# The first unit of the long convolutions, placed between the last input projections

## The chip, the cores and the metric

The program runs on one core of a Trainium2 chip. Five engines work side by side and meet at semaphores: TensorE (PE, matrix products into PSUM), VectorE (DVE), ScalarE (ACT), GpSimd (Pool) and SyncE (SP), of which the last two only issue transfers in the part told of here. The metric is the time of one execution on the device, in microseconds, as the median of several; less is better.

## The reference

The reference is a two-layer model of 1024 tokens by 1024 channels in float32: a mixer and a mixture of experts, then a second block. The change is in the second block, in its branch of long convolutions. There a projection of 3 x 1024 channels goes through a short convolution of 3 taps, is cut into v, x1 and x2, and v is convolved with a filter as long as the sequence, twice, each time multiplied by a gate:

```python
hy = dwconv(hy, conv_b_w[l], conv_b_b[l], (HYENA_CONV // 2, HYENA_CONV - 1 - HYENA_CONV // 2))
v, x1, x2 = jnp.split(hy, HYENA_ORDER + 1, axis=-1)
filt = hyena_filters(S, filt_w1[l], filt_b1[l], filt_w2[l], filt_b2[l], filt_w3[l], filt_freq[l])
z = v.astype(f32)
for n, gate in enumerate((x1, x2)):
    k = bidir_kernel(filt[:, n, 0], filt[:, n, 1])
    z = gate.astype(f32) * fftconv(z, k, filt_bias[l, n])
...
def fftconv(u, k, bias):
    L = u.shape[1]
    U = jnp.fft.rfft(u, n=2 * L, axis=1)
    K = jnp.fft.rfft(k, axis=0)
    y = jnp.fft.irfft(U * K[None], n=2 * L, axis=1)[:, :L]
    return y + u * bias.astype(jnp.float32)
```

## The kernel before

**Input projections** (`hyena_inputs_phase`). 24 tiles of 128 channels, j = 0 to 23; the first 16 hold v and x1, tiles 16 to 23 hold x2. For each tile SP loads 0.5 MB of weights (line 3311), DVE splits them into an upper part and a rest (`split_w`), PE makes the product in 48 matmuls (`wide_product`), ACT copies it to `raw`, DVE makes the three taps of the short convolution in `conv` (lines 3437 and 3442), and Pool stores it (line 3296 for x2). Two buffers of each alternate.

**Filter steps.** After tiles 17 to 22 PE also makes 16 slices of the filters (`make_filter`, 4 matmuls each, two PSUM tiles `turned` in turn), DVE multiplies each by its decay (`decay_filter`, line 4142; the two with t = 0 have two small fixups more) and ACT stores every second one. `STEPS_AFTER` says how many stand after each of the last eight tiles. A step needs the decay of the step two before it.

**Long convolutions** (`hyena_phase`). Four passes: pass 0 and 1 are the first convolution for the two halves of the channels, 2 and 3 the second one. A pass has two halves of the frequencies (fh), and a unit is one such (pass, fh): PE makes four spectra of the input, U(n, fh), each of a chunk `u` that SP loads from memory into one of three buffers (line 4260, 0.5 MB); ACT copies each (line 4408); DVE joins them by butterflies, multiplies by the filter's spectra K and goes through the butterflies of the inverse (lines 3769 to 4500), 34.85 us in all, and counts up `h_ready`. For pass 0, K is loaded (line 4164, 2 MB), for pass 1 it is made on PE too and joined by DVE. With both units of a pass done, PE makes I(n), the inverse transform, in 8 banks of PSUM, and DVE multiplies each bank into a gated result (line 4442); a bank is used again when the result two before it has been taken. Each engine goes through a fixed order:

```python
program = [("U", 0, 0), ("U", 0, 1), ("U", 1, 0), ("K", 1, 0), ("K", 1, 1), ("I", 0, 0), ("U", 1, 1), ("U", 2, 0),
           ("I", 1, 0), ("U", 2, 1), ("U", 3, 0), ("K", 3, 0), ("K", 3, 1), ("U", 3, 1), ("I", 2, 0), ("I", 3, 0)]
```

DVE takes the units in the order (0,0), (0,1), (1,0), (1,1), ... and puts the results of pass 0, numbered 0 to 7 here, between the operations of unit (1,0), those of pass 1 between the operations of (2,0). Below, "unit (0,1)" is DVE's work and "U(0,1)" PE's.

## Time and profile before

| | |
|---|---|
| median of 3 runs | 3959.01 us (3958.61 to 3959.40) |
| the profiled execution's own time | 3965.33 us |
| its span | 3963.4 us |
| PE busy over the span | 3711.4 us (94%) |
| DVE busy | 2842.3 us (72%) |
| ACT, Pool busy | 1856.4 us (47%), 260.6 us (7%) |
| last projection ends, long convolutions begin on PE | 2224.6 us |
| DVE's unit (0,0) | 2239.65 to 2274.50 us |
| I(0) on PE | 2312.1 to 2340.5 us |
| I(1) begins on PE | 2398.7 us |

Times in us are counted from the span's start. The shares of the whole span say little here, since most of it is the two mixtures of experts; the change is in 2138 to 2400 us. An idle time in brackets behind a row of a timeline is that of the engine just before the instruction, with what ended it.

### The profile page before, as it was taken

To read this page: it belongs to the slowest core of one execution; us is meant where nothing else is said; L and a number is where in the kernel's file an instruction comes from. 1 tells how busy PE (TensorE), PEld (TensorE's weight loads), DVE (VectorE), ACT (ScalarE), POOL (GpSimd) and SP (SyncE) were. 2 spreads that over 40 slices of the span, in tenths; PEclk is the share of its full clock that TensorE was granted. 3 is DMA by queue.
4 is the path that set the end of the run, shared out by engine and by line. 5 is a ranking of instruction groups with operands and counts; after the bars stand their busy time and mean duration, and the time that the engine had idled before them with its cause. 6 is when DMAs were issued, how large, how long until landed. Compare 5 with 4: busy or idle time off the path is not lost. (4 is left out here: it accounts for less than half of the span.)

```text
span 3963.4 us, 42184 instructions
## 1 busy us (share of the span) xinstructions
PE 3711.4 (94%) x16780; PEld 2853.8 (72%) x16780; DVE 2842.3 (72%) x2581; ACT 1856.4 (47%) x1719; POOL 260.6 (7%) x281
## 2 busy tenths in 40 slices
PE   8989989799999799999999987899499999999998
...
GB/s 118 6 11 116 22 71 159 321 417 415 417 415 353 228 126 72 67 67 103 95 122 143 201 142 102 53 159 120 192 369 387 383 389 379 390 381 389 388 383 319
DMA packets 367168, 891.04 MB, mean 225 GB/s; under 512 B 21994, under 2 KB 118609, under 8 KB 357556
## 3 DMA queue, kind: packets, MB, share of 16 engines
...
q8 instruction: 97, 1.59, 0.2%
...
## 5 line engine op out<-in xcount | busy, mean ns | idle before, releaser
L2342 DVE TENSOR_TENSOR moe_w_rest<-moe_w_w,moe_upper 128x2048 fp32r<-128x2048 f32 x384 | 862.2, 2287 | 134.5 <-ACT moe_upper L2243 68.5
L2243 ACT ACTIVATE moe_upper<-moe_w_w 128x2048 fp32r<-128x2048 f32 x192 | 357.4, 1909 | 233.3 <-PE moe_y_ps L2207 87.2
L2342 DVE TENSOR_TENSOR moe_w_rest<-moe_w_w,moe_upper_w 128x2048 fp32r<-128x2048 f32 x192 | 430.4, 2282 | 14.5 <-ACT moe_upper_w L2261 14.3
L2261 ACT ACTIVATE moe_upper_w<-moe_w_w 128x2048 fp32r<-128x2048 f32 x192 | 357.5, 1910 | 117.3 <-PE moe_up_ps L2181 72.5
L2251 ACT ACTIVATE moe_upper<-moe_w_w 128x2048 fp32r<-128x2048 f32 x192 | 356.7, 1912 | 3.5 <-DMA moe_w_w<-in_w_up_dram 3.5
L2181 PE MATMUL moe_up_ps<-moe_upper,moe_x_upper 128*128 128x512 f32 x768 | 308.6, 402 | 0.0
L2181 PE MATMUL moe_gate_ps<-moe_upper,moe_x_upper 128*128 128x512 f32 x768 | 300.8, 392 | 4.7 <-DVE moe_x_rest L2355 4.7
L2181 PE MATMUL moe_gate_ps<-moe_upper,moe_x_rest 128*128 128x512 f32 x768 | 300.4, 391 | 0.0
L2181 PE MATMUL moe_gate_ps<-moe_w_rest,moe_x_upper 128*128 128x512 f32 x768 | 300.1, 391 | 0.0
L2181 PE MATMUL moe_up_ps<-moe_upper,moe_x_rest 128*128 128x512 f32 x768 | 300.1, 391 | 0.0
L2181 PE MATMUL moe_up_ps<-moe_w_rest,moe_x_upper 128*128 128x512 f32 x768 | 299.0, 389 | 0.0
L2207 PE MATMUL moe_y_ps<-moe_upper_w,moe_hidT_upper 128*128 128x512 f32 x760 | 295.9, 389 | 1.9 <-DVE moe_hidT_rest L2360 1.9
L2207 PE MATMUL moe_y_ps<-moe_upper_w,moe_hidT_rest 128*128 128x512 f32 x760 | 295.7, 389 | 0.0
L2207 PE MATMUL moe_y_ps<-moe_w_rest,moe_hidT_upper 128*128 128x512 f32 x760 | 295.7, 389 | 0.0
L2181 PEld LDWEIGHTS moe_gate_ps<-moe_upper,moe_x_upper 128*128 128x128 f32 x768 | 145.1, 189 | 35.7 <-DVE moe_x_rest L2355 5.5
L2181 PEld LDWEIGHTS moe_up_ps<-moe_upper,moe_x_rest 128*128 128x128 f32 x768 | 144.1, 188 | 31.9
L2181 PEld LDWEIGHTS moe_gate_ps<-moe_upper,moe_x_rest 128*128 128x128 f32 x768 | 145.0, 189 | 30.3
L2181 PEld LDWEIGHTS moe_gate_ps<-moe_w_rest,moe_x_upper 128*128 128x128 f32 x768 | 145.2, 189 | 30.1
L2207 PEld LDWEIGHTS moe_y_ps<-moe_upper_w,moe_hidT_upper 128*128 128x128 f32 x760 | 142.6, 188 | 32.2 <-DVE moe_hidT_rest L2360 2.7
L2181 PEld LDWEIGHTS moe_up_ps<-moe_w_rest,moe_x_upper 128*128 128x128 f32 x768 | 144.6, 188 | 27.5
L2207 PEld LDWEIGHTS moe_y_ps<-moe_upper_w,moe_hidT_rest 128*128 128x128 f32 x760 | 142.7, 188 | 29.6
L2207 PEld LDWEIGHTS moe_y_ps<-moe_w_rest,moe_hidT_upper 128*128 128x128 f32 x760 | 142.7, 188 | 29.5
...
## 6 DMA issues: line engine op xcount, KB each, us to landing
...
moe_w_w<-in_w_up_dram SPq DMA_DIRECT2D x64, 2048.0 KB, 11.0
moe_w_w<-in_w_down_dram SPq DMA_DIRECT2D x64, 2048.0 KB, 10.9
...
```

Of the source, the lines that this page charges most:

```text
L2181: last = nc.tensor.matmul(out[:, :], lhs[:, k, :], rhs[:, k, :], start=(k == 0 and n == 0), stop=(k == ND - 1 and n == 2))
L2207: last = nc.tensor.matmul(m.y_ps[:, h, :], lhs[:, k, :], rhs[:, k, bass.ts(h, BANK)], start=(start and k == 0 and n == 0), stop=(stop and ...
L2243: act.activation(half(upper1(c), h), half(weights.w1[c % 2], h), ACT.Copy).then_inc(m.w1_rounded, 1)
L2251: act.activation(half(upper3(c), h), half(weights.w3[c % 2], h), ACT.Copy).then_inc(m.w3_rounded, 1)
L2261: act.activation(half(upper2(i, c), h), half(weights.w2[c % 2], h), ACT.Copy).then_inc(m.w2_rounded, 1)
L2342: dve.tensor_tensor(half(rest, h), half(whole, h), half(upper, h).bitcast(F32), ALU.subtract).then_inc(done, 1)
```

## The change

The unit (0,0) is made inside the projections. The filter steps are set to four after each of tiles 17 to 20 and none after 21 and 22. After them PE makes U(0,0) into the same two PSUM tiles `turned` that the filter steps use, ACT copies it to `first_U`, and DVE makes the unit ahead of the convolutions of tiles 21, 22 and 23, of which the one of 21 and the split of the last weights stand inside it. `first_U` lies where the filter's operand was, `first_K` where the decay was, and `first_cross` in `rows`. SP loads first_K and, once the first spectrum is made, the fourth chunk. Semaphores of the long convolutions are made earlier, Pool waits for the first unit before its first gates, and the load of the inverse's table waits for the first unit's products. The body of the butterflies became a function, `unit_butterflies`, with the same instructions.

```diff
-            for i in range(N_NAT // 2 + 1, N_ALL // 2):
-                load(i)
-                next_tables.load_rows(sp, v_x1, i - N_NAT // 2 - 1)
+            load(N_NAT // 2 + 1)
+            for b in range(2):
+                next_tables.load_rows(sp, v_x1, b)
+            load(N_NAT // 2 + 2)
+            next_tables.load_rows(sp, v_x1, 2)
+            next_tables.load_first_k(sp)
+            load(N_NAT // 2 + 3, [0])
+            next_tables.load_last_rows(sp, v_x1)
+            load(N_NAT // 2 + 3, [1])
...
                             next_tables.make_filter(pe, s, turned_ps[s % 2])
+                        if j == N_NAT + UNIT_AFTER:
+                            next_tables.first_spectra(pe, turned_ps)
...
                             next_tables.store_filter(act, s, kept_of(s))
+                        if j == N_NAT + UNIT_AFTER:
+                            next_tables.copy_first(act, turned_ps)
...
+            def last_tiles(unit):
+                LAST = N_ALL - 1
+
+                def between(at):
+                    if at == 4:
+                        split_w(LAST, LAST // 2, 1)
+                    elif at == 5:
+                        convolve(LAST - 2, (LAST - 2) // 2, 1, False)
+                split_w(LAST - 1, LAST // 2, 0)
+                for b in NB:
+
+                    dve.wait_ge(next_tables.filt_stored[b], 16 * (NT // 2))
+                dve.wait_ge(next_tables.fwd_copied, RADIX)
+                unit_butterflies(unit, next_tables, 0, next_tables.first_K[:, :, :, :], next_tables.first_U[:, :, :, :], first_cross[:, :, :, :], HC,
+                                 (next_tables.k_loaded[0], 16), between, False)
+                convolve(LAST - 1, LAST // 2, 0, False)
+                convolve(LAST, LAST // 2, 1, False)
...
-STEPS_AFTER = (0, 3, 3, 3, 3, 2, 2, 0)
+STEPS_AFTER = (0, 4, 4, 4, 4, 0, 0, 0)
+UNIT_AFTER = 4
...
-        sp.wait_ge(m.filt_ready, len(FILTER_STEPS))
+        sp.wait_ge(m.product_ready, 1)
         sp.dma_start(m.inv[:, :, :, :, :], m.inverse).then_inc(m.inv_loaded, 16)
...
+    def load_first_k(m, sp):
+
+        sp.wait_ge(m.filt_ready, len(FILTER_STEPS))
+        sp.dma_start(m.first_K[:, :, :, :], m.spectra[PASSES[0][0], 0]).then_inc(m.k_loaded[0], 16)
+
+    def load_last_rows(m, sp, v_x1):
+
+        sp.wait_ge(m.fwd_made, 1)
+        sp.dma_start(m.u[0][:, :, :], residues(v_x1, RESIDUE[RADIX - 1], 0)).then_inc(m.u_loaded[0], 16)
+
+    def first_spectra(m, pe, outs):
+
+        pe.wait_ge(m.tr_loaded, 16 * HJ)
+        pe.wait_ge(m.filt_ready, len(FILTER_STEPS))
+        for i in range(RADIX):
+            pe.wait_ge(m.u_loaded[i % N_CHUNKS], 16 * (i // N_CHUNKS + 1))
+            if i >= 2:
+
+                pe.wait_ge(m.fwd_copied, i - 1)
...
-            if what == "U":
+            if what == "U" and (n, fh) != (0, 0):
...
-        pool.wait_ge(fwd_made, RADIX)
+        pool.wait_ge(h_ready, 1)
```

On VectorE, before: the convolutions of the last two tiles; now: what follows the convolution of tile 20 (`block_w_first` and `hyin_w` are the two weight buffers, the first holds even tiles; `hyin_conv` is a convolution). Before:

```order
L3437 TENSOR_SCALAR hyin_conv<-hyin_raw,hyin_vec 128x1024
L3442 SCALAR_TENSOR_TENSOR hyin_conv<-hyin_raw,hyin_vec,hyin_conv 128x1024 x2
L3437 TENSOR_SCALAR hyin_conv<-hyin_raw,hyin_vec 128x1024
L3442 SCALAR_TENSOR_TENSOR hyin_conv<-hyin_raw,hyin_vec,hyin_conv 128x1024 x2
L4416 UNCONDITIONAL_BRANCH
L3769 TENSOR_TENSOR hyena_U<-hyena_U 128x2x1024
L3774 SCALAR_TENSOR_TENSOR hyena_U<-hyena_U 128x2x1024
```

Now, from the split of tile 22's weights to the middle of the unit:

```order
L130 CAST block_w_first_upper<-block_w_first 128x1024
L133 TENSOR_TENSOR block_w_first_rest<-block_w_first,block_w_first_upper 128x1024
L3813 TENSOR_TENSOR hytab_first_U<-hytab_first_U 128x2x1024
L3818 SCALAR_TENSOR_TENSOR hytab_first_U<-hytab_first_U 128x2x1024
L3813 TENSOR_TENSOR hytab_first_U<-hytab_first_U 128x1024
L3818 SCALAR_TENSOR_TENSOR hytab_first_U<-hytab_first_U 128x1024
L4260 TENSOR_TENSOR hytab_first_U<-hytab_first_U 128x512
L3813 TENSOR_TENSOR hytab_first_U<-hytab_first_U 128x512
L3818 SCALAR_TENSOR_TENSOR hytab_first_U<-hytab_first_U 128x512 x2
L4285 TENSOR_TENSOR hyin_first_cross<-hytab_first_U,hytab_first_K 128x2048
L130 CAST hyin_w_upper<-hyin_w 128x1024
L133 TENSOR_TENSOR hyin_w_rest<-hyin_w,hyin_w_upper 128x1024
```

The unit stood behind the last two convolutions, which now stand behind it; the split of tile 23's weights came before the convolution of tile 22 and is now inside the unit.

On SP, the transfers from the weights of tile 20 to the second unit's chunks (`hytab_u` is a chunk of the input, `tmp_spectra` the filter's spectra in memory). Before:

```order
L3311 DMA block_w_first<-in_w_in_dram 128x8x128
L3311 DMA hyin_w<-in_w_in_dram 128x8x128
L4161 DMA hytab_u<-tmp_v_x 128x2x512
L3311 DMA block_w_first<-in_w_in_dram 128x8x128
L3311 DMA hyin_w<-in_w_in_dram 128x8x128
L4161 DMA hytab_u<-tmp_v_x 128x2x512
L4245 UNCONDITIONAL_BRANCH
L4260 DMA hytab_u<-tmp_v_x 128x2x512
L4164 DMA hyena_K<-tmp_spectra 128x4096
L4260 DMA hytab_u<-tmp_v_x 128x2x512 x4
```

Now:

```order
L3314 DMA block_w_first<-in_w_in_dram 128x8x128
L3314 DMA hyin_w<-in_w_in_dram 128x8x128
L4213 DMA hytab_u<-tmp_v_x 128x2x512
L4218 DMA hytab_first_K<-tmp_spectra 128x4096
L3314 DMA block_w_first<-in_w_in_dram 128x8x128
L4223 DMA hytab_u<-tmp_v_x 128x2x512
L3314 DMA hyin_w<-in_w_in_dram 128x8x128
L4378 UNCONDITIONAL_BRANCH
L4391 DMA hytab_u<-tmp_v_x 128x2x512 x4
L4245 DMA hyena_K<-tmp_spectra 128x4096
```

The fourth chunk of U(0,0) stood ahead of the 2 MB of spectra and now stands behind them and behind the weights of tile 22.

On PE, where the filter steps of tile 20 end (L4179 and L4180 are `make_filter`, L2751 the projection of tile 21), now:

```order
L4179 MATMUL hyin_turned<-hytab_w_parts_14099,hytab_hid_upper 128x512
L4180 MATMUL hyin_turned<-hytab_w_parts_14099,hytab_hid_rest 128x512
L4179 MATMUL hyin_turned<-hytab_w_parts_14099,hytab_hid_upper 128x512
L4180 MATMUL hyin_turned<-hytab_w_parts_14099,hytab_hid_rest 128x512
L4236 MATMUL hyin_turned<-hytab_u,hytab_tr 128x512 x16
L2751 MATMUL hyin_proj<-block_h_T_upper,hyin_w_upper 128x512
L2751 MATMUL hyin_proj<-block_h_T_rest,hyin_w_upper 128x512
```

The 16 matmuls of U(0,0) stood behind the projection of tile 23 before, at the head of those of line 4328.

## Rows read from the trace of the kernel before

**Rows 1.** Busy time by stretch; columns in its first line.

```profile
core 0: us, PE busy (x) PEld busy (x) DVE busy (x) ACT busy (x) POOL busy (x), PEclk, DMA share, GB/s
2138.50:2224.70 86.20, 83.03 (x354) 67.03 (x353) 50.54 (x48) 6.17 (x6) 3.21 (x6) 0.98 0.38 134
...
2239.70:2312.10 72.40, 69.04 (x160) 30.43 (x161) 70.62 (x55) 15.36 (x15) 1.46 (x2) 1.00 0.39 144
...
2342.80:2398.70 55.90, 25.34 (x60) 10.88 (x58) 54.45 (x46) 8.19 (x8) 1.45 (x2) 0.76 0.56 207
```

**Rows 2.** Waits of PE from 2138 to 2560 us: total, times, longest.

```profile
PE hyena_inv_ps L4366 <- DVE hyena_U L4500: 30.6, 1, 30.6
...
PE hyin_turned L4127 <- DVE hyin_rows L4142: 0.9, 2, 0.5
```

**Rows 3.** Timeline of PE: start, length, line, count, idle before it.

```profile
2224.56 13.90 PE L4328 MATMUL hyena_fwd_ps<-hytab_u,hytab_tr 128*128 128x512 f32 x32
2240.22 14.00 PE L4328 MATMUL hyena_fwd_ps<-hytab_u,hytab_tr 128*128 128x512 f32 x32 [1.76 <-DMA hytab_u<-tmp_v_x]
2257.06 14.00 PE L4328 MATMUL hyena_fwd_ps<-hytab_u,hytab_tr 128*128 128x512 f32 x32 [2.84 <-DMA hytab_u<-tmp_v_x]
...
2312.10 7.03 PE L4366 MATMUL hyena_inv_ps<-hyena_U,hytab_inv 128*128 128x512 f32 x16
2319.81 20.87 PE L4366 MATMUL hyena_inv_ps<-hyena_U,hytab_inv 128*128 128x512 f32 x48 [0.68 <-DVE hyena_z L4442]
2340.52 10.03 PE L4328 MATMUL hyena_fwd_ps<-hytab_u,hytab_tr 128*128 128x512 f32 x23
```

**Rows 4.** Timeline of DVE, last tile and first unit, then results 0 and 7.

```profile
2226.67 2.61 DVE L3442 SCALAR_TENSOR_TENSOR hyin_conv<-hyin_raw,hyin_vec,hyin_conv 128x1024 f32<-128x1024 f32 x2
2239.65 2.29 DVE L3769 TENSOR_TENSOR hyena_U<-hyena_U 128x2048 f32<-128x2048 f32 x1 [10.38 <-ACT hyena_U L4408]
...
2249.72 2.29 DVE L4480 TENSOR_TENSOR hyena_cross<-hyena_U,hyena_K 128x2048 f32<-128x2048 f32 x1
...
2273.81 0.69 DVE L4500 SCALAR_TENSOR_TENSOR hyena_U<-hyena_U 128x512 f32<-128x512 f32 x1
...
2319.06 0.69 DVE L4442 TENSOR_TENSOR hyena_z<-hyena_inv_ps,hyena_z 128x512 f32<-128x512 f32 x1
...
2342.82 0.69 DVE L4442 TENSOR_TENSOR hyena_z<-hyena_inv_ps,hyena_z 128x512 f32<-128x512 f32 x1
```

**Rows 5.** Timeline of PE: projection 17, then the first filter steps.

```profile
2127.47 0.48 PE L2751 MATMUL hyin_proj<-block_h_T_upper,hyin_w_upper 128*128 128x512 f32 x1
...
2138.45 0.39 PE L4127 MATMUL hyin_turned<-hytab_w_parts,hytab_hid_upper 128*128 128x512 f32 x1
...
2142.35 0.50 PE L4127 MATMUL hyin_turned<-hytab_w_parts,hytab_hid_upper 128*128 128x512 f32 x1 [1.90 <-DVE hytab_filt L4147]
...
2143.61 0.63 PE L2751 MATMUL hyin_proj<-block_h_T_upper,block_w_first_upper 128*128 128x512 f32 x1
```

**Rows 6.** Timeline of DVE, decays of the filter steps.

```profile
2144.18 0.68 DVE L4147 SCALAR_TENSOR_TENSOR hyin_rows<-hyin_rows,hytab_bias 1x512 f32<-1x512 f32 x1
...
2159.64 1.23 DVE L4142 TENSOR_TENSOR hyin_rows<-hyin_turned,hytab_decay 128x1024 f32<-128x1024 f32 x1 [0.23 <-PE hyin_turned L4128]
```

**Rows 7.** Busy time by stretch, columns as in Rows 1.

```profile
2144.00:2146.00 2.00, 2.00 (x6) 1.59 (x5) 1.97 (x4) 0.00 (x0) 0.00 (x0) 0.50 0.00 0
2254.00:2258.00 4.00, 1.16 (x3) 0.49 (x3) 3.90 (x4) 1.02 (x1) 0.00 (x0) 1.00 0.68 226
```

**Rows 8.** Timeline of SP, issues of the two spectra loads of the first pass.

```profile
2228.60 0.47 SPq L4164 DMA_DIRECT2D hyena_K<-tmp_spectra  x1
...
2244.36 0.47 SPq L4164 DMA_DIRECT2D hyena_K<-tmp_spectra  x1
```

**Rows 9.** Landing times of the stores of a finished tile (line 3296).

```profile
DMA to landing us min/median/max: 2.9/3.1/9.2
```

**Rows 10.** Landing times of the input chunks loaded at line 4260.

```profile
DMA to landing us min/median/max: 3.6/4.7/17.9
```

More of the change, by code:

```diff
@@ L3261, in hyena_inputs_phase @@
         nat = v_x1.rearrange("(t p) c -> p t c", p=P)
+        unit = []
         def steps_after(j):
@@ L3303, in _, with load @@
         def _(sp):
-            def load(i):
-                for b in NB:
+            def load(i, tiles=NB):
+                for b in tiles:
                     j = 2 * i + b
@@ L3415, in _, with convolve @@
             ends = Chain(dve, next_tables.end_step)
+            def convolve(j, i, b, turning):
+                dve.wait_ge(raw_ready, j + 1)
+                if not first(i):
+                    if turning:
+                        dve.wait_ge(turned, j - 1)
+                    else:
+                        dve.wait_ge(stored[b], 16 * i)
+                dve.tensor_scalar(conv[b][:, :], raw[b][:, 0:T], vec[:, bass.ds(j, 1)], vec[:, bass.ds(j + R_BIAS, 1)],
+                                  ALU.mult, ALU.add).then_inc(tap_done, 1)
+                for k in range(1, HY_TAPS):
+                    dve.wait_ge(tap_done, (HY_TAPS - 1) * j + k)
+                    dve.scalar_tensor_tensor(conv[b][:, :], raw[b][:, k:k + T], vec[:, bass.ds(j + k * N_ALL, 1)], conv[b][:, :],
+                                             ALU.mult, ALU.add).then_inc(conv_ready if k == HY_TAPS - 1 else tap_done, 1)
             def two_tiles(i, turning):
@@ L3419, in two_tiles @@
                     j = 2 * i + b
-                    if not first(j) and not (isinstance(j, int) and j == N_ALL - 1):
+                    if not first(j):
                         split_w(j + 1, i + b, 1 - b)
@@ L3449, in _ @@
             next_tables.sum_weights(dve)
-            for i in range(N_NAT // 2, N_ALL // 2):
+            for i in range(N_NAT // 2, N_NAT // 2 + 2):
                 two_tiles(i, False)
-        return Ends(proj_made, N_ALL, raw_ready, N_ALL, conv_ready, N_ALL, rows_ready, N_NAT, stored, 16 * (N_ALL // 2))
+            split_w(N_ALL - 3, N_NAT // 2 + 2, 1)
+            for s in steps_after(N_ALL - 4):
+                next_tables.decay_filter(ends, s, turned_ps[s % 2], kept_of(s))
+            convolve(N_ALL - 4, N_NAT // 2 + 2, 0, False)
+            unit.append(Chain(dve, next_tables.step))
+            last_tiles(unit[0])
+        return Ends(proj_made, N_ALL, raw_ready, N_ALL, conv_ready, N_ALL, rows_ready, N_NAT, stored, 16 * (N_ALL // 2), unit[0])
 class MergeStore(Store):
@@ L4063, in open @@
         m.k_loaded = [m.sem(f"k_loaded{fh}") for fh in range(HF)]
+        m.fwd_made = m.sem("fwd_made")
+        m.fwd_copied = m.sem("fwd_copied")
+        m.product_ready = m.sem("product_ready")
+        m.h_ready = m.sem("h_ready")
+        m.step = m.sem("step")
         return m
@@ L4167, with unit_butterflies, add, sub @@
 N_U = 3
+COS_OF, SIN_OF = (C0, C1, C2, C3), (S0, S1, S2, S3)
+def unit_butterflies(c, tab, g, k, x, by, width, k_ready, between, last_half):
+    dve = c.engine
+    def add(x, y):
+        add_to(c, x, y)
+    def sub(x, y):
+        c.then(dve.tensor_tensor(x, x, y, ALU.subtract))
+    def twice(x, y, sign, op):
+        twice_and(c, x, y, sign, op)
+    add(x[:, 0:3:2], x[:, 1:4:2])
+    between(0)
+    if width == HC:
+        twice(x[:, 1:4:2], x[:, 0:3:2], -1, ALU.add)
+    else:
+        twice(x[:, 1], x[:, 0], -1, ALU.add)
+        twice(x[:, 3], x[:, 2], -1, ALU.add)
+    between(1)
+    add(x[:, 0], x[:, 2])
+    twice(x[:, 2], x[:, 0], -1, ALU.add)
+    between(2)
+    sub(x[:, 1, RE], x[:, 3, IM])
+    add(x[:, 1, IM], x[:, 3, RE])
+    twice(x[:, 3, IM], x[:, 1, RE], 1, ALU.add)
+    twice(x[:, 3, RE], x[:, 1, IM], -1, ALU.add)
+    between(3)
+    if k_ready:
+        dve.wait_ge(*k_ready)
+    for s in range(2):
+        kx, xx = k[:, 2 * s:2 * s + 2], x[:, 2 * s:2 * s + 2]
+        c.then(dve.tensor_tensor(by, xx[:, :, ::-1, :], kx[:, :, IM:IM + 1, :].to_broadcast([P, 2, 2, width]), ALU.mult))
+        between(4 + 2 * s)
+        last = dve.tensor_tensor(xx, xx, kx[:, :, RE:RE + 1, :].to_broadcast([P, 2, 2, width]), ALU.mult)
+        if s == 1 and not last_half:
+            last.then_inc(tab.product_ready, 1)
+            dve.wait_ge(tab.product_ready, g + 1)
+        else:
+            c.then(last)
+        between(5 + 2 * s)
+        sub(xx[:, :, RE, :], by[:, :, RE, :])
+        add(xx[:, :, IM, :], by[:, :, IM, :])
+    add(x[:, 0], x[:, 2])
+    twice(x[:, 2], x[:, 0], -1, ALU.add)
+    add(x[:, 1], x[:, 3, ::-1])
+    twice(x[:, 3], x[:, 1, ::-1], -1, ALU.add)
+    add(x[:, 0], x[:, 1])
+    twice(x[:, 1], x[:, 0], -1, ALU.add)
+    add(x[:, 2, RE], x[:, 3, RE])
+    sub(x[:, 2, IM], x[:, 3, IM])
+    twice(x[:, 3, RE], x[:, 2, RE], -1, ALU.add)
+    dve.scalar_tensor_tensor(x[:, 3, IM], x[:, 3, IM], 2.0, x[:, 2, IM], ALU.mult, ALU.add).then_inc(tab.h_ready, 1)
 class HyenaStore(Store):
@@ L4417, in _ @@
     def _(dve):
-        c = Chain(dve, step)
-        def add(x, y):
-            add_to(c, x, y)
-        def sub(x, y):
-            c.then(dve.tensor_tensor(x, x, y, ALU.subtract))
-        def twice(x, y, sign, op):
-            twice_and(c, x, y, sign, op)
+        c = inputs.unit
         def result(n, bank):
@@ L4505, in _ @@
             dve.wait_ge(inputs.stored[b], inputs.n_stored)
-        butterflies(0, 0, None)
         for n in range(1, NP):
```

91 lines of the change are left out of this document (26 added, 65 removed).

## The prediction

> **What bounds the kernel now.** I read the busy time by stretch first, then the waits, then the timelines of TensorE (PE) and VectorE (DVE). The change touches the stretch from the last input projections (2138 us) to the first inverse transform. From 2239.7 to 2312.1 us DVE is busy 70.62 of 72.40 us and PE 69.04 of 72.40: both are full [rows 1]. From 2342.8 to 2398.7 DVE has 54.45 of 55.90 us while PE has 25.34 [rows 1]. In that last stretch PE waits 30.6 us for the h_ready of the fourth unit, which DVE makes [rows 2]. So the bound after 2343 us is DVE, and a time saved there counts only if DVE reaches 2343 us earlier.
>
> What stands just before that point decides the case. I(0), the inverse transform of pass 0, starts on PE at 2312.10 and makes 8 banks, DVE multiplies each into z, the last at 2342.82 [rows 3, 4]. PE didn't wait before I(0): no idle time is noted at 2312.10 [rows 3]. DVE had both units of pass 0 done by 2309.2 (two units of 34.85 us from 2239.65). Hence I(0) starts when PE is through its own queue, not when DVE is. A bank takes (2340.52 - 2319.81) / 6 = 3.45 us, and PE waits once, 0.68 us, for DVE's first result at 2319.06 [rows 3, 4]. Bank 0 was made at about 2315.6, so DVE was 3.5 us behind PE at result 0; bank 7 was made at 2340.5, so DVE was 2.3 us behind at result 7. These 2.3 us are all that a faster DVE can gain here.
>
> **DVE's part of the change.** The first unit (2239.65 to 2274.50, 34.85 us) [rows 4] leaves the stretch after the projections and goes between them, where DVE is busy only 50.54 of 86.20 us [rows 1]. The work is the same; it is hidden by projections 21 to 23, three times 10.9 us on PE (projection 17 took 2127.47 to 2138.45) [rows 5]. What it drags along: the convolutions of tiles 22 and 23 (0.84 + 2.61 us each, [rows 4] shows the second part) now stand behind it. I put U(0,0)'s copies at 2213.4 (below); 12.4 us of the unit (2239.65 to 2252.04, the end of the first cross product) [rows 4] end at 2225.8; the split of tile 23 waits for its weights, about 1.5 us, and ends at 2229.2, 5 us before PE wants it; then 2.3 + 3.5 + 20.1 us of unit and of convolution 21, and 7 us of the last two convolutions: 2262. The store of tile 23 lands 3.1 to 9.2 us after its issue [rows 9] and DVE waits for it before unit (0,1): start 2266 to 2272 in place of 2274.5. Its end is at 2301 to 2307, and with the filter butterflies of pass 1 and the first addition (9.9 us, from 2309.19 to the first result at 2319.06) DVE stands ready for result 0 at 2311 to 2317. Bank 0 is made at 2319.6 (below), so DVE waits 3 to 9 us for PE. ScalarE's first copy of U(1,0), about 2264.7, waits for the last convolution (2262): covered by 2.6 us, and by two PSUM buffers more.
>
> **PE's part.** The matmuls are the same in number, so the start of I(0) moves by waits alone. Each in turn:
> - Four filter steps after tile 17 in place of three. Step 3 reuses the bank that step 1's decay frees at 2144.86 [rows 6], and step 2 is through at 2143.61 [rows 5]: +1.25 us. The granted clock was 0.50 there, its lower level of 1.2 GHz (2144 to 2146, after PE's pause before 2142.35) [rows 5, 7]. Two microseconds at half speed lose 1.0 us, with their edges I estimate 1.4, and leave that unchanged.
> - Four in place of three after tiles 18, 19, 20. Two of the three groups already wait 0.45 us each [rows 2], the third about as much; the fourth step comes 0.1 us before its bank is free: +0.3 us. The groups of two after 21 and 22 go, they had no wait.
> - U(0,0) must now wait until the last decay is done, since it uses the same PSUM. A third decay runs 2159.64 to 2160.87 [rows 6]; a fourth would end at 2162.0, against 2160.4 for the matmuls: +1.6 us. Bounds 1.2 and 2.
> - The fourth chunk of U(0,0) is loaded into the first one's buffer when the first spectrum is made. Before it went to the queue ahead of the 2 MB of spectra and no wait is seen before 2240. Now first_K (2 MB) and the weights of tile 22 (0.5 MB) stand ahead of it on SP's queue. The nearest rows: a chunk queued behind such a load was there 11.6 us (2228.60 to 2240.22) and 12.7 us (2244.36 to 2257.06) after the load was issued [rows 3, 8]. With the weights some 1.5 us more: 13.6 us after 2195.2 is 2208.8, and PE wants it three spectra (10.4 us) after its start at 2195.2, at 2205.6: +3.2 us. Bounds: 0, if it lands in the usual 4.7 us, and 11, if in the worst 17.9 us [rows 10].
> - U(0,1)'s first chunks are loaded during projection 23: the 1.76 us [rows 3] go.
> - U(1,0)'s chunk is still behind 2 MB of spectra: 2.84 us before [rows 3]. Pool's two gate loads (now behind h_ready) no longer lie before it; I keep 2.2: -0.6 us, bounds -2.84 and 0.
>
> Sum: 1.25 + 0.3 + 1.6 + 3.2 - 1.76 - 0.6 = +4.0 us. I(0) starts at 2316.1, now makes its 8 banks without a wait (8 x 3.45 = 27.6 us), and bank 7 is there at 2343.7; DVE takes result 7 at 2344.0 in place of 2342.82: +1.2 us. From there DVE does what it did before, PE has its 30 us of slack, and the rest of the program follows. The profiled run took 3965.33 us for a span of 3963.4, 6.3 us over the median of 3959.01; the difference of 1.2 us applies to either: 3966.5 and 3960.2 us. The moved DVE work, 34.85 us, is thus worth nothing: it turns into a wait of DVE for I(0).
>
> A rule would have it otherwise: the Trainium skill, Perfetto Trace Analysis, section Identifying the Most-Contended Engine, takes the busy share for DVE (98% here) and weight loading for TensorE (42% here, 30.43 of 72.40 [rows 1]), and says to optimize the most contended engine first. By it DVE alone binds the stretch, and what is taken from DVE comes off the time; that is the second rival.
>
> **The rivals.** All of them are placed on the same sum.
> - The small gain. The chunk lands in time (0 for 3.2) and U(1,0) waits no more (-2.84 for -0.6): the sum is -1.4, I(0) starts at 2310.7, result 7 at 2338.6: -4.2 us, 3954.8. For it: a plain chunk lands in 4.7 us. Against: both chunks seen behind spectra were late.
> - DVE alone binds and PE keeps up. Then unit (0,1) begins 2.5 to 11.4 us earlier (2272 or, with all luck, 2263 for 2274.42) and all of it is kept; with the usual store, 7.5 to 11.4: about 3949.5. Against it is that PE has no gap before I(0).
> - The clock. Each new pause of PE brings the lower clock as the one before 2142.35 did, 1.4 us each, three of them: +4.2, 3964.4. Against: after the 2.84 us pause before 2257.06 the clock stayed at 1.00 [rows 7].
> - Slower: the chunk of U(0,0) is stuck behind the 2 MB as long as the worst chunk of the trace, 17.9 us [rows 10]. PE stands 11.0 us in place of 3.2, projections 21 to 23 and I(0) with it, and I(0) hands it to DVE one for one: 1.2 + 7.8 = +9.0 us, 3968.0. It decides from a landing 16.8 us after its issue on.
>
> **How the numbers follow.** 0.2% of this kernel is 7.9 us, about what a measurement of it can tell from no change. My forecast (3958.5 to 3962.5) 0.62, the small gain 0.17, the clock 0.09, DVE alone 0.05, the late chunk 0.07. The first three are all within 0.2%; DVE alone gives faster in four of five cases. So faster 0.04, same 0.89, slower 0.07. The range 3954.5 to 3965 holds the first three cases but for their edges.
>
> **What would show it.** Right: DVE waits 3 to 9 us for hyena_inv_ps before result 0, results follow at PE's 3.45 us, I(0) starts 2 to 6 us later than before relative to tile 17, PE waits about 3 us for hytab_u inside the moved spectra and 1.6 us ahead of them, and the wait for the fourth unit stays near 30 us. Wrong: I(0) starts earlier by more than 2 us, PE waits for h_ready before I(0), a projection waits for its split weights, or the stretch after result 7 changes in length. If DVE reaches result 0 after bank 0 is made, I took its slack too large and the store's landing is the step to look at.

## The result and the profile after

| | before | after |
|---|---|---|
| median, 9 runs each on one chip | 3959.01 us (3957.41 to 3964.52) | 3968.57 us (3963.11 to 3974.82) |
| ratio, 95% interval | | 1.0024 (1.0016 to 1.0032) |
| the profiled execution, its span | 3965.33, 3963.4 us | 3969.61, 3967.7 us |

The changed kernel is slower, by 6.3 to 12.7 us; forecast were +1.2 us and a range up to 3965.0. One execution of the kernel before, in one of the groups used further down, took 4821.64 us at a mean granted clock of 0.742, and the ratios leave it out. Lines have moved: the filter steps are L4179 and L4180, their decays L4194, U(0,0) is L4236, the other spectra L4459, I(n) L4497, a result L4567, the unit's last operation L4305.

PE's timeline after (start, length, line, count, idle before it), from the first filter step to I(1), against [rows 3, 5]:

```profile
2133.70 0.39 PE L4179 MATMUL hyin_turned<-hytab_w_parts,hytab_hid_upper 128*128 128x512 f32 x1
...
2137.60 0.50 PE L4179 MATMUL hyin_turned<-hytab_w_parts,hytab_hid_upper 128*128 128x512 f32 x1 [1.89 <-DVE hytab_filt L4199]
...
2140.16 0.80 PE L4179 MATMUL hyin_turned<-hytab_w_parts,hytab_hid_upper 128*128 128x512 f32 x1 [1.34 <-DVE hyin_rows L4199]
```

The same timeline from the last filter steps on:

```profile
2187.90 0.50 PE L4179 MATMUL hyin_turned<-hytab_w_parts,hytab_hid_upper 128*128 128x512 f32 x1 [0.40 <-DVE hytab_filt L4194]
...
2191.67 10.54 PE L4236 MATMUL hyin_turned<-hytab_u,hytab_tr 128*128 128x512 f32 x24 [1.43 <-issue]
2206.20 5.40 PE L4236 MATMUL hyin_turned<-hytab_u,hytab_tr 128*128 128x512 f32 x8 [4.00 <-DMA hytab_u<-tmp_v_x]
...
2244.11 13.90 PE L4459 MATMUL hyena_fwd_ps<-hytab_u,hytab_tr 128*128 128x512 f32 x32
2258.23 14.00 PE L4459 MATMUL hyena_fwd_ps<-hytab_u,hytab_tr 128*128 128x512 f32 x32 [0.22 <-DMA hytab_u<-tmp_v_x]
2272.07 41.36 PE L4459 MATMUL hyena_fwd_ps<-hytab_filt,hytab_tr 128*128 128x512 f32 x96
2313.27 1.88 PE L4497 MATMUL hyena_inv_ps<-hytab_first_U,hytab_inv 128*128 128x512 f32 x4
...
2398.47 21.91 PE L4497 MATMUL hyena_inv_ps<-hyena_U,hytab_inv 128*128 128x512 f32 x47 [30.10 <-DVE hyena_U L4305]
```

I count from the first filter step, at 2138.45 before and 2133.70 after, since what lies ahead of it is the same program. I(0) starts 179.57 us behind it; before 173.65 (2312.10 - 2138.45). That is +5.9 us; I had forecast +4.0. Every pause that I listed is in these rows: 1.34 us in the fourth step, 1.43 ahead of U(0,0), 4.00 for the fourth chunk; of the two before U(0,1) and U(1,0) [rows 3] the first has gone and the second has shrunk to 0.22. For the 1.43 us the row names no releaser; the last decay, for which U(0,0) waits in the program, ends on DVE at 2191.56.

DVE after, the same columns, against [rows 4]: the unit's first and last operation, unit (0,1), results 0, 5, 6 and 7:

```profile
2212.80 2.29 DVE L3813 TENSOR_TENSOR hytab_first_U<-hytab_first_U 128x2048 f32<-128x2048 f32 x1 [5.96 <-ACT hytab_first_U L4242]
...
2253.91 0.69 DVE L4305 SCALAR_TENSOR_TENSOR hytab_first_U<-hytab_first_U 128x512 f32<-128x512 f32 x1
...
2268.34 2.29 DVE L3813 TENSOR_TENSOR hyena_U<-hyena_U 128x2048 f32<-128x2048 f32 x1 [7.01 <-DMA tmp_x_T<-hyin_conv]
...
2317.00 0.69 DVE L4567 TENSOR_TENSOR hyena_z<-hyena_inv_ps,hyena_z 128x512 f32<-128x512 f32 x1 [4.04 <-PE hyena_inv_ps L4497]
...
2334.17 0.69 DVE L4567 TENSOR_TENSOR hyena_z<-hyena_inv_ps,hyena_z 128x512 f32<-128x512 f32 x1 [0.55 <-PE hyena_inv_ps L4497]
...
2339.61 0.69 DVE L4567 TENSOR_TENSOR hyena_z<-hyena_inv_ps,hyena_z 128x512 f32<-128x512 f32 x1
...
2342.54 0.69 DVE L4567 TENSOR_TENSOR hyena_z<-hyena_inv_ps,hyena_z 128x512 f32<-128x512 f32 x1
```

The unit went where the diff puts it, and DVE waits 7.01 us for the last store and 4.04 us for I(0) before result 0: the freed time became waits, as forecast. Result 7 stands 208.84 us behind the first filter step, before 204.37: +4.5 us. From there to I(1) it is 55.93 us, before 55.92, with PE waiting 30.1 us for the fourth unit where it waited 30.6, against [rows 2]:

```profile
PE hyena_inv_ps L4497 <- DVE hyena_U L4305: 30.1, 1, 30.1
...
PE hyin_turned L4236 <- DMA hytab_u<-tmp_v_x: 4.0, 1, 4.0
...
PE hyin_turned L4179 <- DVE hyin_rows L4199: 1.3, 1, 1.3
```

The forecast for I(0) was too low by 1.9 us although the pauses are shorter than forecast; what makes up for them, the granted clock shows (columns as in [rows 1]; the clock is the third number from the end), against [rows 7]:

```profile
2138.00:2144.00 6.00, 4.66 (x13) 3.39 (x12) 4.83 (x6) 0.00 (x0) 0.00 (x0) 0.55 0.51 189
2144.00:2146.00 2.00, 2.00 (x7) 1.52 (x7) 1.93 (x3) 0.00 (x0) 0.00 (x0) 0.64 0.61 232
2146.00:2148.00 2.00, 2.00 (x10) 1.63 (x9) 1.97 (x3) 0.00 (x0) 0.30 (x1) 1.00 0.08 30
...
2208.00:2210.00 2.00, 2.00 (x4) 0.70 (x3) 0.00 (x0) 0.00 (x0) 0.00 (x0) 0.50 0.00 0
2210.00:2212.00 2.00, 2.00 (x7) 1.17 (x6) 0.00 (x0) 0.36 (x1) 0.00 (x0) 0.92 0.00 0
```

Busy time over the whole stretch, from the first filter step to I(0), after:

```profile
2133.70:2313.30 179.60, 169.53 (x546) 104.19 (x545) 131.60 (x110) 26.66 (x26) 5.20 (x9) 0.97 0.40 143
```

And before:

```profile
2138.40:2312.10 173.70, 165.93 (x545) 103.25 (x545) 124.59 (x106) 26.64 (x26) 5.20 (x9) 0.99 0.41 148
```

PE has the lower clock (0.50, 1.2 GHz) through the fourth filter step and to about 2145.4 (0.55 over 6 us and 0.64 over 2 are some 6.8 us at the lower level; before it was 3.4), and again at 2208, behind the 4.00 us pause, where 8 matmuls take 5.40 us; the 24 before them took 10.54, that is 3.5 for 8. Over the whole stretch the same matmuls keep PE busy 169.53 us in place of 165.93, at a mean clock of 0.97 in place of 0.99: +3.6 us of the 5.9 are matmuls that took longer, +2.3 are pauses. My estimate from these rows is that 2.8 of the 3.6 are the clock: after, 8.9 us of matmuls ran at half speed (6.8 less the pause of 1.34, and 3.4), before 3.4, and half of the difference is lost. The other 0.8 I put down to the restarts behind pauses, of which there are two more; that is not shown.

### The profile page after: what moved, and what is told of

It reads as the page before. It is cut to its first block and busy times, and to the rows that moved or that the text cites. A ratio compares the mean times of both kernels' runs of the same rounds, so it can differ in the third digit from the quotient of the medians.

```text
span 3967.7 us, 42186 instructions
## 1 busy us (share of the span) xinstructions
PE 3711.8 (94%) x16780; PEld 2855.3 (72%) x16780; DVE 2843.0 (72%) x2581; ACT 1856.8 (47%) x1719; POOL 264.6 (7%) x281
## 5 line engine op out<-in xcount | busy, mean ns | idle before, releaser
L2181 PEld LDWEIGHTS moe_gate_ps<-moe_w_rest,moe_x_upper 128*128 128x128 f32 x768 | 145.2, 189 | 30.1
```

The lines of the kernel that those rows point to most:

```text
L2181: last = nc.tensor.matmul(out[:, :], lhs[:, k, :], rhs[:, k, :], start=(k == 0 and n == 0), stop=(k == ND - 1 and n == 2))
```

## The experiments

Times in the table are us from the first filter step of each trace; the stretch is the same program in all. Medians are of 10 to 11 runs (9 for before and after, 5 for inverse_early_before). A ratio compares with the runs of before in the same group: before 3958.88, 3959.63 and 3959.61 us in the three groups of experiments. It is taken over all the runs and can differ in the fourth digit from the quotient of two medians.

| kernel | U(0,0) | I(0) | result 7 | I(1) | median | ratio, interval |
|---|---|---|---|---|---|---|
| before | 86.1 | 173.65 | 204.37 | 260.3 | 3959.01 | |
| before_again | 84.5 | 171.14 | 202.74 | 258.7 | 3960.20 | 1.0004 (0.9994 to 1.0013) |
| after | 58.0 | 179.57 | 208.84 | 264.8 | 3968.57 | 1.0024 (1.0016 to 1.0032) |
| after_again | 57.7 | 178.81 | 208.07 | 264.0 | 3965.92 | 1.0020 (1.0011 to 1.0029) |
| no_unit | 84.4 | 174.84 | 204.10 | 260.0 | 3959.81 | 1.0005 (0.9995 to 1.0014) |
| steps4 | 89.0 | 175.69 | 207.28 | 263.2 | 3963.46 | 1.0014 (1.0005 to 1.0023) |
| chunk_first | 57.1 | 172.45 | 201.72 | 257.6 | 3961.66 | 1.0007 (0.9998 to 1.0016) |
| steps_3445 | 56.2 | 178.65 | 207.92 | 263.9 | 3962.82 | 1.0010 (1.0000 to 1.0019) |
| inverse_early | 57.7 | 162.60 | 196.01 | 264.3 | 3970.97 | 1.0025 (1.0016 to 1.0034) |
| inverse_early_before | 84.4 | 169.31 | 202.71 | 271.0 | 3976.49 | 1.0040 (1.0025 to 1.0054) |
| split_chunk_first | 57.1 | 166.96 | 201.55 | 257.5 | 3959.72 | 0.9993 (0.9983 to 1.0004) |
| split_all | 56.2 | 166.40 | 199.81 | 255.7 | 3957.79 | 0.9992 (0.9983 to 1.0001) |
| split_before | 86.1 | 170.95 | 204.35 | 260.3 | 3959.65 | 0.9997 (0.9988 to 1.0006) |
| split_after | 57.6 | 172.22 | 205.65 | 261.6 | 3962.12 | 1.0003 (0.9994 to 1.0012) |

**The same two kernels again.**

> The changed kernel once more, unaltered. Its runs so far lie in three groups (3963 to 3964, 3968 to 3971, 3974 to 3975 us), those of the kernel before in two (3957 to 3960, 3964). Theory A: the change costs about 4.5 us in its own stretch (up to result 7 of the first inverse transform, read against the start of the first filter step), and what is over that is the lower clock striking here and there in other stages, some 1.7 us at a time. Then the group of the fastest runs stays at 3963 to 3964 us and the stretch costs 4 to 6 us again. Theory B: all 9.6 us are caused in the stretch or just behind it; then the trace shows 8 to 10 us between the start of the first filter step and the start of the router's stage.

> The kernel before once more, nothing edited: how far two profiled executions of one program differ, stretch by stretch. Theory A (what the changed kernel loses lies between the first filter step and result 7; what differs upstream and downstream is chance): the ratio is 1.000 within 0.001; the stretch from the first filter step to result 7 is 204.4 us again within 0.5, and that from result 7 to the end (1620.6 in the first trace) comes out anywhere from 1618 to 1625. Rival (the 2 to 4 us that the changed kernel's traces lose behind result 7 belong to it): 1618 to 1621 here.

The loss repeats: 1.0020. The trace has the same two stretches at the lower clock and I(0) at 178.81. Result 7 is 3.7 us later than in the first trace of before and 5.3 later than in the second (4 to 6 were expected), and the fastest run, 3960.52 us, lies below the 3963 that theory A gave as the floor. The kernel before varies more than I had thought: result 7 is at 202.74, not within 0.5 us of 204.4, and its second trace has the 1.90 us pause of the first filter steps and no lower clock behind it. Behind result 7 it takes 1619.8 us, which both theories allow. PE's timeline at the pause and the busy time by stretch of before_again, behind PE's pause; in the first trace the clock was 0.50 there [rows 7]:

```profile
2139.78 0.50 PE L4127 MATMUL hyin_turned<-hytab_w_parts,hytab_hid_upper 128*128 128x512 f32 x1 [1.90 <-DVE hytab_filt L4147]
```

```profile
2139.00:2142.00 3.00, 2.22 (x10) 1.84 (x11) 2.90 (x5) 0.00 (x0) 0.00 (x0) 1.00 0.57 207
2142.00:2146.00 4.00, 4.00 (x19) 3.34 (x18) 3.93 (x5) 0.00 (x0) 0.00 (x0) 1.00 0.35 131
```

So the lower clock behind one and the same pause comes in one execution and not in another. I(0) differs by 2.5 us between two traces of the kernel before: 1.6 of them are there at U(0,0), by this clock, and 1.1 come from the pause ahead of U(1,0), 1.74 us for 2.84. The changed kernel is then 7.2 us later at I(0) than the mean of them (172.4).

**What DVE's work was worth.** In no_unit, the kernel before, DVE leaves the butterflies and products of unit (0,0) out:

```diff
-        butterflies(0, 0, None)
+        dve.wait_ge(fwd_copied, u_made(0, 0))
+        dve.wait_ge(tab.k_loaded[0], 16)
+        dve.tensor_scalar(cross[:, 0, 0, 0:2], U_of(0, 0)[:, 0, 0, 0:2], 1.0, None, ALU.mult).then_inc(product_ready, 1)
+        dve.wait_ge(product_ready, 1)
+        dve.tensor_scalar(cross[:, 0, 0, 2:4], U_of(0, 0)[:, 0, 0, 2:4], 1.0, None, ALU.mult).then_inc(h_ready, 1)
```

> The kernel before, with VectorE's work of the unit (0,0) left out (34.85 us of butterflies and products; the spectra are made and copied, and two instructions on two columns give the signals), so its output is not the reference's. It prices a VectorE that is freed of the whole unit. Theory A (TensorE's queue sets the start of the first inverse transform): result 7 comes 2.1 to 2.3 us earlier, the time is 3956 to 3958 us. Rival (VectorE alone binds the stretch): 20 to 35 us less, 3924 to 3939 us.

DVE's timeline of no_unit, the second unit, the filter butterflies, results 0 and 7:

```profile
2252.29 2.29 DVE L3769 TENSOR_TENSOR hyena_U<-hyena_U 128x2048 f32<-128x2048 f32 x1 [14.93 <-ACT hyena_U L4408]
...
2292.86 1.22 DVE L3769 TENSOR_TENSOR hyena_K<-hyena_K 128x1024 f32<-128x1024 f32 x1 [5.72 <-ACT hyena_K L4408]
...
2315.94 0.69 DVE L4442 TENSOR_TENSOR hyena_z<-hyena_inv_ps,hyena_z 128x512 f32<-128x512 f32 x1 [13.23 <-PE hyena_inv_ps L4366]
...
2341.47 0.69 DVE L4442 TENSOR_TENSOR hyena_z<-hyena_inv_ps,hyena_z 128x512 f32<-128x512 f32 x1
```

Without the 34.85 us nothing is faster: 1.0005. DVE waits 14.93 us for U(0,1), 5.72 for K(1,0) and 13.23 for I(0). This refutes the rival by which DVE alone binds. The 2.1 to 2.3 us that theory A expected are not there either: result 7 is at 204.10. Here PE's own chain was late, since the lower clock came behind its pause of 2.90 us ahead of U(1,0), where the first trace of before has 2.84 us and keeps 1.00 [rows 3, 7]. PE's timeline and the busy time by stretch of no_unit there:

```profile
2254.10 17.07 PE L4328 MATMUL hyena_fwd_ps<-hytab_u,hytab_tr 128*128 128x512 f32 x32 [2.90 <-DMA hytab_u<-tmp_v_x]
```
```profile
2254.00:2258.00 4.00, 3.90 (x5) 1.84 (x6) 3.93 (x3) 0.00 (x0) 0.00 (x0) 0.50 0.16 61
```

The 32 matmuls take 17.07 us for 14.00. The run also shows the two chains that meet at result 7. With unit (0,0) on DVE behind the projections, result 7 comes 118.27 us behind the start of U(0,0) in all five traces (204.37 - 86.11 and the like), wherever I(0) starts: DVE sets it. Without it there, result 7 comes 29.26 or 29.27 us behind I(0) (no_unit, after, after_again, chunk_first, steps_3445): PE sets it. Before the change PE's chain would have ended at 173.65 + 29.27 = 202.9, DVE's at 204.4. By this sum 1.5 us of slack, 2.3 in before_again (200.4 for 202.7), were all there was to gain; the change took these and gave PE more than that to wait for.

**The steps and the chunk, one at a time.** steps4 is the kernel before with STEPS_AFTER of the changed one and with the changed one's wait of DVE for a store ahead of one decay; chunk_first and steps_3445 are the changed kernel with one edit each, this one

```diff
-            next_tables.load_first_k(sp)
             load(N_NAT // 2 + 3, [0])
             next_tables.load_last_rows(sp, v_x1)
+            next_tables.load_first_k(sp)
```

and this one:

```diff
-STEPS_AFTER = (0, 4, 4, 4, 4, 0, 0, 0)
+STEPS_AFTER = (0, 3, 4, 4, 5, 0, 0, 0)
```

> The kernel before with one part of the change alone: four filter steps after each of tiles 17 to 20 and none after 21 and 22. Theory A: TensorE loses 1.3 us before the fourth step, 0.3 us at the other groups and about 1.3 us to a longer stretch at the lower clock after them, and since the first unit starts with it, the whole moves: +2 to +4 us, 3961 to 3963 us. Rival: the steps are free, their waits only take the place of others: 3958.5 to 3959.5 us.

> The changed kernel with the fourth chunk of U(0,0) put on SP's queue ahead of the 2 MB of first_K, and behind the weights of tile 22 only. Theory A: the chunk lands about 5 us after its issue, TensorE's 4.0 us wait inside the spectra goes and with it the lower clock behind it (1.7 us). The first inverse transform starts 5 to 6 us earlier, result 7 comes 4 to 5.5 us earlier, the time is 3957 to 3960 us in its fastest group, no more than 1 us from the kernel before. Rival (the cost lies in the filter steps or behind the stretch): less than 2 us gained against the changed kernel.

> The changed kernel with three filter steps after tile 17, as before, four after 18 and 19 and five after 20. Theory A (PE's new pause of 1.3 us in the fourth step, and the lower clock that stays twice as long there, are 2.6 us of the 5.9 by which I(0) starts late): the pause goes, a second short one of 0.4 us comes in the group of five, I(0) starts 177.0 us after the first filter step in place of 179.6 and 178.8, result 7 stands at 206.0 in place of 208.8 and 208.1, the time is 3963.5. Rival (the pause moves to the group of five, since a fifth step waits for the decay of the third as the fourth did): I(0) at 178.5 to 179.5 and 3966 us as in the changed kernel.

SP's issues after, and in chunk_first:

```profile
2191.59 0.34 SPq L4218 DMA_DIRECT2D hytab_first_K<-tmp_spectra  x1
2191.98 0.43 SPq L3314 DMA_DIRECT2D block_w_first<-in_w_in_dram  x1
2195.37 0.59 SPq L4223 DMA_DIRECT2D hytab_u<-tmp_v_x  x1
```
```profile
2185.80 0.37 SPq L3314 DMA_DIRECT2D block_w_first<-in_w_in_dram  x1
2195.47 0.37 SPq L4223 DMA_DIRECT2D hytab_u<-tmp_v_x  x1
2195.88 0.47 SPq L4218 DMA_DIRECT2D hytab_first_K<-tmp_spectra  x1
```

Behind the 2 MB the chunk is there 10.83 us after its issue (2206.20 - 2195.37). Ahead of them PE makes all 32 matmuls in one piece:

```profile
2191.76 13.97 PE L4236 MATMUL hyin_turned<-hytab_u,hytab_tr 128*128 128x512 f32 x32 [1.44 <-issue]
...
2238.25 27.85 PE L4459 MATMUL hyena_fwd_ps<-hytab_u,hytab_tr 128*128 128x512 f32 x64
```

The pause and the lower clock behind it are gone. I(0) and result 7 come 6.4 to 7.1 us earlier than in the changed kernel, and the ratio falls from 1.0020 to 1.0007 (their intervals overlap; the medians, of one group, are 4.3 us apart). Of the 6.4 to 7.1 us 0.6 to 0.9 are there at U(0,0) already and are not the chunk's: the lower clock at the fourth filter step lasted 3.4 us in this execution, not 6.8. The other 5.7 to 6.2 us are the larger part of the loss. 4.0 us of them are the wait, 1.7 the clock (one stretch of 3.4 us at half speed).

steps4 alone costs 1.0014, with U(0,0) 2.9 to 4.5 us later: the step's pause of 1.31 us and 6.8 us at the lower clock, for 3.4 and none in the two traces of before. In steps_3445 the pause in the fourth step goes and the clock is low half as long there. U(0,0) starts 1.5 to 1.8 us earlier. But the wait for the chunk grows and the lower clock behind it lasts twice as long:

PE's timeline and the busy time by stretch of steps_3445 there:

```profile
2206.14 6.28 PE L4236 MATMUL hyin_turned<-hytab_u,hytab_tr 128*128 128x512 f32 x8 [4.35 <-DMA hytab_u<-tmp_v_x]
```
```profile
2206.00:2210.00 4.00, 3.86 (x5) 1.79 (x6) 0.77 (x1) 0.00 (x0) 0.00 (x0) 0.50 0.01 4
2210.00:2212.00 2.00, 2.00 (x5) 0.75 (x4) 0.00 (x0) 0.00 (x0) 0.00 (x0) 0.66 0.00 0
```

I(0) is at 178.65, not at the 177.0 expected: neither theory had it right, the pause did not move, but its gain was paid at the next wait. The median, 3962.8, is 3 us lower than after_again's; the intervals overlap, and the trace does not show the gain.

**Can DVE's freed time be used?** If PE's queue sets the start of I(0), then I(0) has to stand further ahead in it. In inverse_early (on chunk_first) and inverse_early_before (on before) the order is:

```diff
-... ("K", 1, 0), ("K", 1, 1), ("I", 0, 0), ("U", 1, 1)
+... ("K", 1, 0), ("I", 0, 0), ("K", 1, 1), ("U", 1, 1)
```

> The kernel with the fourth chunk ahead of the spectra (chunk_first), and on PE the inverse transform I(0) ahead of the filter spectra K(1,1) in place of behind them. Theory A (PE's own queue sets the start of I(0), DVE has been ready 4.5 us before result 0): I(0) starts as soon as unit (0,1) is ready, some 162 us after the first filter step in place of 172.5, after an idle time of PE of 3 to 4 us; result 0 comes at 172 in place of 176.2, result 7 at 195.5 in place of 201.7. K(1,1) and U(1,1) then come late for unit (1,1), which waits about 3 us, so that I(1) starts at 254 to 255 in place of 257.6 and the time is 3658 plus 300, that is 3958 to 3959, for 3961.7 of chunk_first. Rival (DVE is behind anyway, its work between the results sets their pace): result 7 and I(1) stay within 1 us of chunk_first and the time at 3961.7.

> The kernel before with the same exchange alone: I(0) ahead of K(1,1). Theory A (before the change DVE is only 3 us ahead of PE at I(0), so the exchange has nothing to win there and K(1,1) and U(1,1) come later): PE waits about 11 us for unit (0,1), I(0) starts at 170.8 us after the first filter step in place of 173.7, result 7 at 202 to 204 in place of 204.4, U(1,1) is some 11 us late and unit (1,1) waits for it, I(1) starts at 262 to 263 in place of 260.3: 3961 us. Rival (K(1,1) has room enough): I(1) starts 2 to 3 us earlier, 3956.5 us.

PE's timeline of inverse_early at I(0) and K(1,1), and DVE's at unit (1,1):

```profile
2296.44 3.75 PE L4497 MATMUL hyena_inv_ps<-hytab_first_U,hytab_inv 128*128 128x512 f32 x4 [9.84 <-DVE hyena_U L4305]
...
2327.54 20.76 PE L4459 MATMUL hyena_fwd_ps<-hytab_filt,hytab_tr 128*128 128x512 f32 x48
```
```profile
2349.40 1.23 DVE L3813 TENSOR_TENSOR hyena_K<-hyena_K 128x1024 f32<-128x1024 f32 x1 [6.00 <-ACT hyena_K L4542]
...
2363.20 2.29 DVE L3813 TENSOR_TENSOR hyena_U<-hyena_U 128x2048 f32<-128x2048 f32 x1 [6.28 <-ACT hyena_U L4542]
```

I(0) and result 7 came where theory A put them (162.6 for 162, 196.0 for 195.5), and still I(1) is 6.6 us later than in chunk_first. In that expectation I had taken K(1,1) for 14 us of PE; two of its four spectra take twice as many matmuls as the others, all four 20.6 us. So PE stood 9.84 us with nothing to do (3 to 4 were expected), and then DVE waited 6.00 and 6.28 us for K(1,1) and U(1,1). The queue up to U(1,1) is full of work that DVE wants soon after: time that PE stands anywhere in it comes back. The same exchange before the change costs 1.0040: I(0) is at 169.3 and result 7 at 202.7, near theory A, but I(1) at 271.0 and not at 262 to 263.

The finer cut moves only the last spectrum of K(1,1), 6.9 us, behind I(0) (`filter_spectra` now gets the slots that it makes as an argument):

```diff
-                filter_spectra(n, fh)
+                filter_spectra(n, fh, SLOTS[:3] if (n, fh) == (1, 1) else SLOTS)
...
                 results(n)
+                if n == 0:
+                    filter_spectra(1, 1, SLOTS[3:])
```

split_chunk_first has it on chunk_first, split_all on that with the steps 3, 4, 4, 5, split_before on before, split_after on the changed kernel.

> The kernel with the fourth chunk ahead of the spectra (chunk_first), and on PE the last of the four filter spectra K(1,1), 6.9 us of its 20.6, moved behind I(0); the other three stay ahead. Theory A (up to U(1,1) PE's queue is the bound; DVE is ready for result 0 4.5 us early, and can be given these without making PE wait): I(0) starts 165.6 us after the first filter step in place of 172.5, without idle time; result 0 comes at 171.7 in place of 176.2, the eight results at DVE's own pace, result 7 at 195.5 in place of 201.7; K(1,1) is whole at 200.3 and U(1,1) copied at 214.9, both before unit (1,1) wants them (208.5 and 216.5), so that I(1) starts at 251.3 in place of 257.6. Time 3955.5 us for 3961.7. Rival (what is won at I(0) is lost at U(1,1) again, as when all of K(1,1) was moved): I(1) at 257 to 259 and 3961 us.

> As split_chunk_first, with three, four, four and five filter steps after tiles 17 to 20. Theory A (the chunk is in time, so that the 1.6 us which three steps after tile 17 brought at the start of U(0,0) are not given back to the wait for the chunk as they were in steps_3445): U(0,0) starts at 56.0 us after the first filter step, all that follows stands 1.1 to 1.6 us earlier than in split_chunk_first, I(1) at 249.9, the time is 3954. Rival (the lower clock falls elsewhere): the same as split_chunk_first within 0.5 us.

> The kernel before with the same split of K(1,1) alone. Theory A (without the moved unit DVE has nothing to spare at I(0)): PE gets to I(0) 6.9 us earlier but waits 3 to 4 us for unit (0,1), and DVE, behind PE already, wins at most the 2.9 us between its second unit and I(0): result 7 at 201.5 to 204 us after the first filter step (204.4 and 202.7 without the split), I(1) within 1.5 us of before (260.3, 258.7), 3958 to 3960 us. Rival (the split alone brings the gain, with the unit moved or not): result 7 and I(1) 5 us or more earlier, 3954 us.

> The changed kernel with the split of K(1,1) alone, the chunk still behind the spectra. Theory A (the start of I(0) on PE is all that keeps the changed kernel from using what the move freed on DVE): I(0) starts some 172.4 us after the first filter step in place of 179.2, result 0 at 179.3 in place of 183.3, result 7 at 202.9 in place of 208.8, I(1) at 258.5 in place of 264.6; the time is 3960 us for 3966 to 3968. Rival (DVE's slack before result 0 belongs to the late chunk): result 7 within 2 us of the changed kernel's and 3966 us.

PE's timeline of split_chunk_first at banks 0 and 2:

```profile
2303.14 1.95 PE L4497 MATMUL hyena_inv_ps<-hytab_first_U,hytab_inv 128*128 128x512 f32 x4 [1.19 <-DVE hyena_U L4305]
...
2313.53 3.68 PE L4497 MATMUL hyena_inv_ps<-hytab_first_U,hytab_inv 128*128 128x512 f32 x4 [3.29 <-DVE hyena_z L4569]
```

And of split_all at bank 2:

```profile
2310.07 1.99 PE L4497 MATMUL hyena_inv_ps<-hytab_first_U,hytab_inv 128*128 128x512 f32 x4 [3.29 <-DVE hyena_z L4569]
```

DVE's timeline at unit (0,1), in split_chunk_first:

```profile
2268.13 2.29 DVE L3813 TENSOR_TENSOR hyena_U<-hyena_U 128x2048 f32<-128x2048 f32 x1 [11.06 <-DMA tmp_x_T<-hyin_conv]
```

And in chunk_first:

```profile
2261.77 2.29 DVE L3813 TENSOR_TENSOR hyena_U<-hyena_U 128x2048 f32<-128x2048 f32 x1 [6.76 <-DMA tmp_x_T<-hyin_conv]
```

The gain stayed away in split_chunk_first (result 7 at 201.55 and I(1) at 257.48, for 195.5 and 251.3 expected): I(0) at 166.96 now waits for unit (0,1), which began late, since the last store of x2 took 4.3 us longer to land than in chunk_first (DVE waits 11.06 us for it in place of 6.76). Why it did is not shown. In this kernel, as in inverse_early, that wait counts; where I(0) stands at the end of the queue it is covered by the wait for I(0). DVE is then not ready for result 0, PE pauses 3.29 us ahead of bank 2, and 4 matmuls take 3.68 us behind it in place of 1.88: the lower clock once more. In split_all the same pause of 3.29 us has no lower clock behind it (1.99). split_all, with a wait of 11.70 us for the store, has result 7 at 199.8, 2.9 to 4.6 us ahead of before, split_after 205.7 for 208.8 and 208.1, and split_before nothing (204.35, for 204.37 in the first trace of before): the split is worth something only where the unit was moved, as theory A has it, but 2.4 to 3.2 us and not 6 in the changed kernel, and 0.2 us in split_chunk_first for 201.72 without it. In these traces it is worth less than each expectation had it. By time all three are near before: 0.9993, 0.9992, 1.0003. None is shown to be faster than the kernel before; split_all's interval ends at 1.0001, so what it may be worth is under 0.2%. Two of the 11 runs of split_chunk_first and two of split_all, at 3948.7 to 3950.0 us, lie 3 us and more below every run of the kernel before (lowest 3953.1); none of them was traced, so what they had is not known. split_after is at 1.0003 where after_again is at 1.0020.

**What stays open.** From result 7 to the end of the span it is 1620.6 us before and 1625.2 after. In the traces whose queue is otherwise theirs it is 1618.0 to 1623.0 with the unit behind the projections (before, before_again, no_unit, steps4, split_before) and 1622.0 to 1627.0 with it moved (after, after_again, chunk_first, steps_3445 and the other three split kernels). Two places in it vary. In I(3), from its first result to its eighth, the eight traces with the unit moved take 0.7 to 2.5 us more than the 34.3 us of the first trace, the six without it from 1.7 less to 1.3 more. Busy time by stretch over it, before_again and then after:

```profile
2552.70:2585.40 32.70, 22.84 (x98) 19.54 (x99) 29.61 (x33) 7.07 (x7) 0.00 (x0) 0.90 0.00 1
```
```profile
2557.60:2593.80 36.20, 26.34 (x99) 22.11 (x100) 29.80 (x34) 7.07 (x7) 0.00 (x0) 0.81 0.00 0
```

What varies there is the clock: it is 0.90 in before_again and steps4 (32.7 and 32.6 us), 0.85 in before (34.3), 0.81 in after (36.2), 0.77 in split_after and split_chunk_first (36.6 and 36.7). Behind the last large tiles of the mixture of experts the end takes 2.1 us longer in after, but also 2.5 in before_again, so the second place is no property of the change. Whether the lower clock in I(3) is one was not tried. As means of the two traces of each kernel, result 7 is 4.9 us later after the change, and the stretch behind it 3.4 us longer; the medians differ by 7 to 9.6. So 2 to 5 us of the loss have no cause shown here.

## Why the prediction was wrong

- **PE sets I(0), DVE's unit is worth nothing:** right, shown by no_unit and by the 4.04 us that DVE waits.
- **The pauses of PE:** right as a sum and somewhat too high. Measured after less before: fourth step 1.34 for 1.25, groups -0.07 for +0.3, ahead of U(0,0) 1.43 for 1.6, chunk 4.00 for 3.2, U(0,1) -1.76, U(1,0) -2.62 for -0.6. Together +2.3 us for +4.0. The chunk was there 14.6 us after the load of first_K was issued (13.6 forecast); the chunk of U(1,0) came 0.22 us late and not 2.2. That the sum is 1.7 us too high hid part of the next error.
- **The clock:** this is the step that failed. I wrote that the lower clock at 2144 stays as it was, and put the rest in a rival at 0.09, speaking against it with the one pause of 2.84 us behind which the clock stayed up. Of the +5.9 us at I(0), 3.6 are matmuls that took longer, some 2.8 of them by the clock: it was low for 6.8 us in place of 3.4 around the fourth filter step, and for 3.4 us more behind the chunk. Behind the third new pause, 1.43 us ahead of U(0,0), it stayed up. A trace in which the pause of 1.90 us brings the lower clock and that of 2.84 us doesn't tells that a pause of this size may or may not bring it, so each new one should have carried part of the price, and the chance of 0.09 had no reason. The very pause that I had put against it, ahead of U(1,0), has the lower clock behind it in no_unit (2.90 us).
- **From I(0) to result 7:** 27.9 us forecast, 29.27 measured. I let DVE take result 7 0.3 us after bank 7, but between results 5 and 7 its own operations of unit (1,0) take longer than the banks, also when it starts punctually: results 5, 6 and 7 are at 2334.17, 2339.61 and 2342.54. What a faster DVE could win back in the trace that I worked from was 1.5 us, not 2.3. Pauses -1.7, matmuls +3.6 and this +1.4 are the 3.3 us between the forecast +1.2 and the measured +4.5 at result 7.
- **After result 7:** the stretch to I(1) is unchanged as forecast (55.93 us, PE waiting 30.1). +4.5 us at result 7 is what the profiled executions show at the end too (+4.3). The medians are 7 to 9.6 apart; the first trace of before was one of its slower executions (6.3 us above its median). I carried the difference over to a median without asking whether that trace had lost at the clock what an average one doesn't: its I(0) was 2.5 us later than in the second. The term for what comes behind I(1) was nothing; the traces have 3.4 us there, and I(3), the one place in it that was looked into, shows a lower clock and no cause for it.

The order of the rivals fell out wrong. In mechanism the clock rival, 4.0 + 4.2 us at I(0) and 3964.4, was nearest. In number the slow rival's 3968.0 is nearest to 3968.57, but by luck: it had the chunk land 17.9 us after its issue and PE stand 11.0 us, and it was there after 10.83 and PE stood 4.00. The place of a good part of the loss, the chunk behind the spectra, was that rival's. The Trainium skill (Perfetto Trace Analysis, section Identifying the Most-Contended Engine) has the most contended engine optimized first, judged by the busy share for DVE and by MFU (the matmuls' share of the peak rate) and the share of weight loading for TensorE. By the shares that the prediction compares, 98% and 42%, that is DVE; it left MFU out. The run of no_unit disagrees: all of 34.85 us taken from DVE give a ratio of 1.0005.
